# RWKV recurrence: chunks seven steps apart instead of six, state-space groups every third step, level masks by predicated copies on DVE

## The reference, cut to what matters

```
RWKV-7, per head (8 heads, state 64 x 64), per token:
    sa = s @ a_t
    s  = s * w_t + sa (x) b_t + v_t (x) k_t
    y  = s @ r_t
S5, per group (32 groups, 16 channels, 64 complex states), per token:
    h = abar * h + B u_t
    y = Re(C h) + D u_t, then gelu
```

## Time and profile before

| | |
|---|---|
| median of 3 runs | 3435.6 us (3430.29 to 3436.28) |
| profiled execution, span | 3435.7 us, no other time is given for it |
| busy: PE, DVE, ACT, POOL | 2925.4, 2208.9, 1236.1, 880.0 us |
| the stage with the change | 683.5 to 1297.0 us of the span |
| in it L1847 on POOL | 160 operations, 144.8 us |
| in it L1833 on DVE | 160 operations, 0.42 us each |

### The profile page before, as it was taken

One profiled execution on the slowest core, in us unless ns is written; L12 is line 12 of the kernel. 1 busy time (PEld: TensorE's weight loads), 2 busy tenths in 40 slices (PEclk: granted clock), 3 DMA queues, 4 the chain that ended last, 5 costly groups with the idle time before them and its releaser, 6 DMA issues. The chain is left out here.

```text
span 3435.7 us, 77289 instructions
## 1 busy us (share of the span) xinstructions
PE 2925.4 (85%) x31187; PEld 2453.0 (71%) x31187; DVE 2208.9 (64%) x3314; ACT 1236.1 (36%) x2205; POOL 880.0 (26%) x742
## 2 busy tenths in 40 slices
PE   8799999876779791899779999997986898996698
PEld 7699999766667670587679777875765666676576
DVE  3435666476676764687527777632437998895587
ACT  1015555333333330434201010111216888884432
POOL 4100000033233320211121111102114776763221
PEclk9899999888899995899889999998997999998899
DMA  4425455433334334655346999976432101007542
GB/s 161 164 88 149 145 153 154 135 82 87 92 90 114 77 99 114 185 164 157 136 148 208 332 344 329 348 244 193 151 123 100 47 17 63 14 2 193 193 147 87
DMA packets 486316, 500.80 MB, mean 146 GB/s; under 512 B 214273, under 2 KB 381426, under 8 KB 480954
## 3 DMA queue, kind: packets, MB, share of 16 engines
q1 hardware_dynamic: 371162, 332.49, 32.5%
q10 hardware_dynamic: 112752, 159.17, 13.7%
q0 software_dynamic: 2048, 4.20, 0.5%
HBM read 357.55 MB, written 138.41 MB: 144 GB/s over the span
## 5 line engine op out<-in xcount | busy, mean ns | idle before, releaser
L2494 POOL TENSOR_TENSOR sp_att<-sp_beta,sp_left 128x512 f32<-128x512 f32 (+3 forms) x320 | 318.4, 1006 | 195.8 <-DVE sp_left L2450 184.1
L1847 POOL TENSOR_TENSOR rc_ct<-rc_m,rc_lev 128x256 f32<-128x256 f32 x160 | 144.8, 926 | 825.4 <-DVE rc_m L1809 825.4
L102 PE MATMUL po_acc<-po_x_high,po_w_low 128*128 128x412 f32 (+1 forms) x840 | 306.8, 365 | 33.4 <-POOL po_w_low L95 15.2
L102 PE MATMUL pe_acc<-pe_x_high,pe_w_low 128*128 128x412 f32 (+1 forms) x840 | 305.0, 363 | 22.3 <-DVE pe_x_low L95 15.0
L103 PE MATMUL po_acc<-po_x_low,po_w_high 128*128 128x412 f32 (+1 forms) x840 | 299.4, 356 | 0.0
L104 PE MATMUL po_acc<-po_x_high,po_w_high 128*128 128x412 f32 (+1 forms) x840 | 299.1, 356 | 0.0
L104 PE MATMUL pe_acc<-pe_x_high,pe_w_high 128*128 128x412 f32 (+1 forms) x840 | 296.0, 352 | 0.0
L103 PE MATMUL pe_acc<-pe_x_low,pe_w_high 128*128 128x412 f32 (+1 forms) x840 | 295.6, 352 | 0.0
L2450 DVE TENSOR_TENSOR_SCAN sp_left<-sp_z,sp_left,sp_zero 128x512 f32<-128x512 f32 x192 | 235.3, 1266 | 14.1 <-ACT sp_z L2394 12.3
L2181 DVE TENSOR_TENSOR po_work<-po_work,po_q 128x1024 f32<-128x1024 f32 x128 | 174.7, 1365 | 84.4 <-DMA po_work<-in_cache_k 79.1
L102 PEld LDWEIGHTS po_acc<-po_x_high,po_w_low 128*128 128x128 f32 x840 | 162.8, 194 | 81.8 <-ACT po_o L801 30.7
(11 more groups left out here) (450 smaller groups left out, 7323.7 us busy)
## 6 DMA issues: line engine op xcount, KB each, us to landing
po_work<-in_cache_k SPq DMA_DIRECT2D x256, 256.0 KB, 4.9
po_work<-in_cache_v ACTq DMA_DIRECT2D x256, 256.0 KB, 4.7
scratch_ops<-pe_work SPq DMA_DIRECT2D x160, 128.0 KB, 2.2
out_z<-pe_o SPq DMA_DIRECT2D x84, 206.0 KB
out_z<-po_o ACTq DMA_DIRECT2D x84, 206.0 KB
pe_w<-in_w_e SPq DMA_DIRECT2D x21, 512.0 KB
po_w<-in_w_o ACTq DMA_DIRECT2D x21, 512.0 KB
rc_opx<-scratch_ops SPq DMA_DIRECT2D x16, 640.0 KB
```

The costliest lines, as they stand in the source:

```text
L102: pe.matmul(out, ll, rh, start=start, stop=False)
L1847: pool.tensor_tensor(ct[q][:, n].rearrange("p (s g) c -> p s g c", s=2), m4[q][:, :, :, 0, :], spread(lev[:, n + 1, :]), ALU.mult).then_in ...
L2494: pool.tensor_tensor(att[h][:, n % 3, 0:w], be[h][:, n % 4, 0:w], left[h][tile(n) % 2][:, at + 1:at + 1 + w], ALU.mult).then_inc(at_ok[h], 1)
```

## The change

1. `LAG` goes from 6 to 7: chunk c starts in step 7c, the stage has 233 steps. The places where SP's program divided a step by 6 now divide by LAG.
2. The state-space groups come every third step (`STRIDE = 3`), the first batch from step 104, the second from 182. DVE builds no sines and cosines in steps 104 to 151.
3. `rc_ct` and POOL's five products per chunk are gone, with their five semaphores. PE multiplies the whole masked matrix `rc_m` with the inverse so far. DVE, in place of adding the product of the level to the inverse, copies the product into it where the level's mask is set (`copy_predicated`); the masks are int32, and four of five are transposed.

```diff
-    BEGIN, LT, FIRST = 6, 52, (104, 166)
+    BEGIN, LT, FIRST, STRIDE = 6, 52, (104, 182), 3
     def at(self, g):
-        return self.FIRST[g // HG] + 2 * (g % HG)
+        return self.FIRST[g // HG] + self.STRIDE * (g % HG)
...
-        if c == self.LT // 6 + 1:
+        if c == self.LT // LAG + 1:
...
-        if c == self.LT // 6 + 5:
+        if c == self.LT // LAG + 5:
...
-            if max(self.at(g) // 6, self.LT // 6 + 6) == c:
+            if max(self.at(g) // LAG, self.LT // LAG + 6) == c:
                 self.load_x(sp, g)
...
-                if t < self.FIRST[0] or t >= self.FIRST[0] + G:
+                if t < self.FIRST[0] or t >= self.FIRST[0] + self.STRIDE * HG:
...
-FLIGHT, LAG = 3, 6
+FLIGHT, LAG = 3, 7
...
-        ct = four("ct", [P, LEVELS, 4, CH])
...
-        lev, lev0 = s_.sb("lev", [P, 6, CH]), s_.sb("lev0", [P, CH])
+        lev, lev0 = s_.sb("lev", [P, LEVELS, CH], I32), s_.sb("lev0", [P, CH])
...
-                    pe.wait_ge(ct_ok[n], c + 1)
...
-                        pe.matmul(b[half[s], r, col(at, g)], ct[q][half[r], n, 2 * s + g, :], xx[q][half[r], s, g, :],
+                        pe.matmul(b[half[s], r, col(at, g)], m4[q][half[r], s, g, 0, :], xx[q][half[r], s, g, :],
...
-                    dve.tensor_tensor(flat(t), flat(t), b[:, :, 0:2 * CH], ALU.add).then_inc(x_sb[n], 1)
+                    dve.copy_predicated(t, spread(lev[:, n, :]), grouped(b[:, :, 0:2 * CH])).then_inc(x_sb[n], 1)
...
             def phase(c, ph):
-                if ph == M_:
-                    pool.wait_ge(m_sb, c + 1)
-                    part(c, 0)
-                elif ph == KV:
-                    part(c, 1)
-                elif ph == U0:
+                if ph == U0:
...
-                elif ph in (U0 + 1, U0 + 2, U0 + 3):
-                    part(c, ph - U0 + 1)
...
-            "lev64": np.stack([level(m)[:64, :64] for m in (1, 2, 4, 8, 16, 32)], 1)[np.r_[0:64, 0:64]],
+            "lev64": np.stack([level(m)[:64, :64].T for m in (2, 4, 8, 16)] + [level(32)[:64, :64]], 1)[np.r_[0:64, 0:64]],
```

More of the change, by code:

```diff
@@ L1269, in sync_end @@
         for g in range(G):
-            if self.at(g) // 6 >= NCH:
+            if self.at(g) // LAG >= NCH:
                 self.load_x(sp, g)
@@ L1578, in rwkv_chunks @@
         levels = lambda n: [s_.sem(f"{n}{k}") for k in range(LEVELS)]
-        u_pe, u_sb, x_pe, x_sb, ct_ok = (levels(n) for n in ("u_pe", "u_sb", "x_pe", "x_sb", "ct"))
+        u_pe, u_sb, x_pe, x_sb = (levels(n) for n in ("u_pe", "u_sb", "x_pe", "x_sb"))
         wc_in = s_.sem("wc_in")
@@ L3050 @@
            "gla_s": (NS * HD, DK, DV), "y": (COLS, D)}
+MASKS = ("lev64",)
 def constants():
@@ L3148 @@
     arrays = {n: np.ascontiguousarray(v) for n, v in layout({n: np.asarray(v) for n, v in inputs.items()}).items()}
-    arrays.update({n: np.ascontiguousarray(v.astype(np.float32)) for n, v in constants().items()})
+    arrays.update({n: np.ascontiguousarray(v.astype(np.int32 if n in MASKS else np.float32))
+                   for n, v in constants().items()})
     ins = {n: nc.dram_tensor(f"in_{n}", v.shape, mybir.dt.from_np(v.dtype), kind="ExternalInput").ap()
```

## The result

The changed kernel takes 3482.2 us (four runs, 3479.8 to 3486.7) against 3432.9 for the kernel before (four runs, 3428.4 to 3436.3): 1.0145 times as long, 95% interval 1.0129 to 1.016. The forecast was 3419 us and faster; its range ended at 3455.

The account below looks back on a forecast made before the run. In-order DVE was taken as nearest its limit in ordinary steps. Ordinary steps -45 us, table steps -5 and groups +34 made -16, hence 3419 us from 3435.6; range 3368 to 3455.

Parts of the forecast that it names:

- Masks leave POOL: DVE's table and sine/cosine work, slowed by POOL's 160 products: 0.32 us per step, of which 0.07 stays.
- Predicated copy: On DVE, replacing an add of the same shape 160 times: 0.42 us each, no change.
- Ordinary step: 112 steps without groups or table transposes: 2.84 us falls to 2.44, saving 45 us.
- Rival 3: Ordinary steps stay at 2.84 us because DVE's relief buys nothing: +29 us, 3464 us; chance 0.05.
- Table step: 16 steps with PE transposes: a seventh less chunk work, 0.34 us each, 5 us saved.
- The group: State-space groups, now over three steps: 6.25 us each rises to 7.3, costing 34 us over 32 groups.
- one loop per group: Among the groups, DVE scan, chunk copies, PE products and handoffs in one chain: 7.5 us a group.
- Rival 1: The loop through DVE governs the groups: at 8.3 us a group, +16 us, 3452 us; chance 0.10.
- two lower bounds, 7.1 and 7.5: Per group over three steps: 7.1 us from PE's work with the same loss, 7.5 from the loop through DVE.
- DVE's bad step in seven: One step in seven where state, inverse and mask of three chunks fall on DVE: 2.3 us.
- rival 4: Mixed parity fills idle time: ordinary step 2.18 us, group 6.7, -65 us, 3371 us; chance 0.17.

Follow-up runs that it names:

- lag_only: The kernel before with chunks seven steps apart and nothing else, POOL still making the level products: 3450.8 us, 1.006 of the kernel before.
- lag_masks: The changed kernel with groups every second step instead of every third, chunks still seven steps apart: 3461.0 us, 1.0083 of the kernel before.
- store_last: The changed kernel with ACT issuing a chunk's output stores at the end of its step: 3451.5 us, 1.0047 of the kernel before.
- lag_masks_store: lag_masks with a chunk's output stores issued at the end of ACT's step: 3423.0 us, 0.9978 of the kernel before.
- lag_only_store: lag_only with a chunk's output stores issued at the end of ACT's step: 3426.1 us.
- y_later: The changed kernel with a group's output products, gelu and store one step later: 3454.7 us.
- y_later_store: The changed kernel with the edits of store_last and y_later together: 3431.6 us, 0.9996 of the kernel before.

## Why the prediction was wrong

**Where the time went.** From the medians: masks -17 us, seven steps instead of six +44, groups every third step +21, in sum 3482. The split depends on the order: with POOL's products in place seven steps cost 17, and the masks then 10 more, which is inside the spread of lag_only's runs. Putting the stores last takes 38 of the 44 back where groups stand two steps apart; in all four pairs of kernels at seven steps it is worth 23 to 38 us (medians).

1. *Masks leave POOL: gain right, size and place off.* At six steps they bring 17 us, where a quarter of a microsecond per ordinary step gave about 28. The six sine/cosine forms fell from 0.93 to 0.76 us in the mean, where I had expected "near 0.70". The form L1476 shows what is left: 12 of its 14 operations took 0.68 us, the two beside POOL's remaining product 1.76. At seven steps, the case that the prediction was about, the masks bring 3 us with the stores last and nothing with the stores in front.
2. *Predicated copy: right.* 0.440 us for 0.420, 160 times:

```profile
L1831 DVE COPY_PREDICATED rc_xx<-rc_lev,rc_bk 128x256 f32<-128x256 int32 x128 | 56.3, 440 | 189.0 <-PE rc_bk L1745 188.6
```

   None took over 0.454 us. Four began while POOL's remaining product of 1.27 us was under way, and they took 0.450 to 0.454. The Trainium skill (SBUF — State Buffer, "SBUF: two separate sides") has DVE and POOL shut each other out where the DVE instruction has two SBUF inputs; the trace agrees if the destination of a predicated copy is not counted as an input.
3. *Ordinary step: the number right, its composition wrong.* 2.46 for 2.44. But I made it of DVE's busy time plus idle time that shrinks with the chunks, with most of the gain from DVE's relief. In lag_only, with POOL's products in place, the ordinary stretches already take 2.51 us a step (steps 7 to 48, 70 to 97 and 140 to 160, 228.7 us); with the masks as well (lag_masks) 2.47. So nearly all of the fall comes from the distance, which spreads a chunk's work over seven steps instead of six. The stores took part of it back: with them last the step is 2.40 us in store_last and 2.35 in lag_masks_store. That the number came out at 2.46 is thus luck, of a relief put too high and stores and clock left out. Rival 3 (0.05) was nearly right that DVE's relief buys nothing at seven steps, and wrong that the step would then stay at 2.84.
4. *Table step: no gain.* Steps 49 to 69 take 85.5 us; less five ordinary ones that is 4.6 each, as before. The wait for ACT's copy stayed (18.3 to 19.9 us). 5 us were expected. The same 21 steps vary with the granted clock more than with any change: 73.6 us at 0.95 in lag_only_store, 93.3 at 0.71 in y_later.
5. *The group: the step that failed.* "I take 7.3, between both", and it is 9.16. That is 32 x 1.86 = 59 us, the whole error of the stage (656.9 for 597). The sign was the wrong one as well: -16 us were forecast and +49 measured. The 7.3 came from one loop per group, or from PE's work per group. But three steps have three rounds of a chunk's products, copies and handoffs. By my own ordinary step of 2.44 us they take 7.3, so the group's 2.55 us on PE and 1.85 on DVE were to cost no more than the table pieces whose place they took. Put the other way, I priced the added step at 1.05 us (7.3 less 6.25), and it cost 2.9. This does not hang on how far apart the groups stand: in lag_masks, with groups two steps apart, a group and an ordinary step take 5.95 + 2.47 us, which makes the added step 2.2, and the kernel is already 42 of the 63 us above the forecast. No kernel at seven steps came to 7.3; the lowest are 7.9 in the second batch of y_later_store and 5.6 + 2.35 in lag_masks_store.
   Of the 1.86 us two parts are shown by runs: the coincidence of input and output products in one step (0.9 us a group, y_later) and the stores (0.4, store_last). Rival 1 named the place and the direction, but its loop ended at 8.3. That I averaged two lower bounds, 7.1 and 7.5, where the larger one holds, is 0.2 of it. Gelu and its store ahead of the copies was also left out, but ACT's level copies wait for it only 3.5 us in all. Without stores and without the coincidence 8.1 us remain; of these the experiments do not say what is the clock (0.97 granted there, 1.00 before), what is handoff and what instruction gaps.
6. *What was not in the sum at all:* on which engine two phases of different chunks meet. I counted DVE's bad step in seven, and said of ACT only that it would fill gaps (rival 4). The same table for ACT shows phases 15, 8 and 1 in one step, with DMA issues among them. In the changed kernel this is 31 us by the medians. In the two profiled stages it is 27: 13 in the stretches with groups, 9 in steps 49 to 69 around the table steps and 5 in the ordinary ones.

**The granted clock.** The sum had no term for it. In the two batches of groups it was 1.00 before and 0.96 and 0.90 in the changed kernel. That is little of the loss: among the changed kernel's chunk distances with groups, four at full clock are 21.5 us on average and six at 0.85 to 0.93 are 22.0. In ordinary steps it weighs more: in steps 70 to 97 of lag_only_store three chunk distances are 16.0 to 16.1 us at clock 1.00 and one is 17.1 at 0.90. Whole runs of one kernel go with it too: lag_only took 3441 us at a mean clock of 0.937 and 3470 at 0.929, y_later_store 3418 at 0.942 and 3443 at 0.937 or 0.938. So a single profile cannot settle a difference of a few us between two kernels, and the cost of the distance with POOL's masks (17 us, from runs over 29) is less certain than that with predicated ones. What makes the clock fall in one execution and not in another stays open.

## What to carry to other kernels

Before a pipeline written out in steps gets another distance, write down for each engine which phases meet in a step, DMA issues included: what was harmless beside phases of the same kind can stand ahead of a copy that everybody waits for. Spreading a side job over more steps pays only if the step is bound by its work; if the steps are bound by a chain of handoffs, a further step costs nearly its full length (here a group step took 3.1 us with half a group in it and 3.05 with a third). As a check on such a sum, multiply the forecast of a step without the side job by the number of steps: if the side job's stretch comes out no longer, it has been priced at nothing. And take the larger of two lower bounds, not their mean.

## What the runs showed of the hardware

- A store issued by ACT holds that engine's sequence for 0.63 us in the median, and two in a row took 2.29 us once, where twice the median is 1.3; the profile shows ACT's next copy as waiting for "issue".
- A predicated copy of 128 x 256 elements from PSUM with an int32 mask took 0.440 us where an add of the same shape took 0.420, and 0.450 to 0.454 where it began during a product of POOL; a product of 128 x 512 elements with both inputs in SBUF went from 0.68 to 1.76 us beside one.
- Four pairs of kernels at seven steps, with the same instructions and only the stores' place in ACT's order changed, differ by 23 to 38 us; the order of instructions in one engine was worth more than the removal of 145 us of POOL work (17 us at six steps, 3 or nothing at seven).
- The granted clock of PE, as a mean over the whole run, lay between 0.929 and 0.943 in these kernels. Within lag_only the run at 0.929 took 29 us longer than the one at 0.937.
